# Eight expert units of a top-2 expert layer: wide and small units in turn, or woven chunk by chunk with one load queue each

## The reference

```python
def _moe(h, w_router, w_gate, w_up, w_down):
    logits = (x @ w_router).astype(jnp.float32)
    top_v, top_i = lax.top_k(logits, TOP_K)
    gates = jax.nn.softmax(top_v, axis=-1)
    combine = jnp.sum(jax.nn.one_hot(top_i, N_EXPERTS) * gates[..., None], axis=1)
    for e in range(N_EXPERTS):
        out = out + combine[:, e:e + 1] * _swiglu(x, w_gate[e], w_up[e], w_down[e])
```

## Time and profile before

| | |
|---|---|
| Time, median of 3 runs | 1328.16 us (1327.37 to 1329.48) |
| The profiled execution's own time | 1328.74 us |
| Its span in the trace | 1326.8 us, so 1.94 us lie outside the span |
| Expert layer on PE | from 480.6 us to 1315.6 us |
| PE busy | 1304.6 us (98%) |
| DVE, ACT busy | 795.7 us (60%), 642.6 us (48%) |
| Bytes moved by DMA | 425.50 MB, 321 GB/s over the span |
| Share of the chain that ended last | PE 84%, DVE 9%, ACT 3% |

### The profile page before, as it was taken

One profiled execution on the slowest core, in us unless ns is written; L12 is line 12 of the kernel. 1 busy time (PEld: TensorE's weight loads), 2 busy tenths in 40 slices (PEclk: granted clock), 3 DMA queues, 4 the chain that ended last, 5 costly groups with the idle time before them and its releaser, 6 DMA issues.

```text
span 1326.8 us, 18843 instructions
## 1 busy us (share of the span) xinstructions
PE 1304.6 (98%) x7654; PEld 983.3 (74%) x7654; DVE 795.7 (60%) x957; ACT 642.6 (48%) x672; POOL 4.5 (0%) x12
## 2 busy tenths in 40 slices
PE   9999999999999999999999999999999999999996
PEld 8999999999999977884448885347887345888332
DVE  7564765653888679972129884118885215888122
ACT  6655644352576587761027772017774005776001
POOL 0000000000000000000000000000000000000000
PEclk9999999999999999999999999999999999999998
DMA  7335354463333499999999999999999999999995
GB/s 299 136 128 190 127 191 159 159 220 140 115 143 128 169 377 341 348 376 405 409 411 426 428 427 426 427 399 426 426 427 427 427 405 427 427 427 426 427 426 227
DMA packets 72347, 425.50 MB, mean 321 GB/s; under 512 B 6384, under 2 KB 8432, under 8 KB 27328
## 3 DMA queue, kind: packets, MB, share of 16 engines
q1 hardware_dynamic: 71680, 422.67, 78.7%
q0 software_dynamic: 432, 1.54, 0.3%
q10 hardware_dynamic: 144, 0.02, 0.0%
HBM read 423.16 MB, written 1.05 MB: 320 GB/s over the span
## 4 chain that ended last, share of the span: by engine, by line
PE 84%; DVE 9%; ACT 3%; issue 3%; DMA 1%; SPq 0%; DVEq 0%; ACTq 0%
PE ps L2388 14%; PE ps L2259 7%; PE ps L2260 7%; PE ps L2265 7%; PE ps L2419 7%; PE ps L1720 5%; PE ps L1710 4%; PE ps L1711 4%; PE ps L2284 4%; PE ps L2285 4%; PE ps L2292 4%; PE ps L1758 2%; PE ps L1775 2%; PE ps L1759 2%; DVE wl L1173 1%
## 5 line engine op out<-in xcount | busy, mean ns | idle before, releaser
L1383 DVE TENSOR_TENSOR wl<-raw,wh 128x2048 fp32r<-128x2048 f32 x96 | 218.6, 2289 | 23.9 <-ACT wh L855 23.8
L855 ACT CAST wh<-raw 128x2048 fp32r<-128x2048 f32 x96 | 183.9, 1916 | 66.8 <-PE ps L2260 40.3
L2259 PE MATMUL ps<-wh,gh 128*128 128x512 f32 x448 | 175.3, 391 | 0.7 <-DVE gl L1457 0.7
L2260 PE MATMUL ps<-wh,gl 128*128 128x512 f32 x448 | 174.4, 389 | 0.0
L918 ACT ACTIVATE sil<-ps 64x512 f32<-64x512 f32 x28 | 16.5, 589 | 299.2 <-PE ps L2390 299.2
L2388 PE MATMUL ps<-raw,few 128*64 128x512 f32 x288 | 130.2, 597 | 0.6 <-DMA raw<-in_moe_w_up 0.6
L2390 PE MATMUL ps<-raw,few 128*64 128x512 f32 x288 | 129.5, 597 | 0.0
L2265 PE MATMUL ps<-wl,gh 128*128 128x512 f32 x448 | 119.8, 389 | 0.0
L1596 DVE COPY few_act<-ps 128x256 f32<-128x256 f32 x28 | 11.9, 425 | 177.9 <-PE ps L2402 177.9
L1047 DVE TENSOR_TENSOR wl<-raw,wh 128x4096 fp32r<-128x4096 f32 (+1 forms) x18 | 73.2, 4069 | 61.7 <-ACT wh L614 39.7
L614 ACT CAST wh<-raw 128x4096 fp32r<-128x4096 f32 (+2 forms) x29 | 92.0, 3173 | 34.5 <-PE ps L1711 34.1
(11 more groups left out here) (343 smaller groups left out, 2692.0 us busy)
## 6 DMA issues: line engine op xcount, KB each, us to landing
raw<-in_moe_w_up SPq DMA_DIRECT2D x71, 1024.0 KB, 12.1
raw<-in_moe_w_gate SPq DMA_DIRECT2D x70, 1024.0 KB, 12.1
raw<-in_moe_w_down SPq DMA_DIRECT2D x51, 1024.0 KB, 13.6
unsplit<-in_moe_w_down SPq DMA_DIRECT2D x33, 1024.0 KB, 10.6
unsplit<-in_moe_w_up SPq DMA_DIRECT2D x25, 1024.0 KB, 14.2
unsplit<-in_moe_w_gate SPq DMA_DIRECT2D x22, 1024.0 KB, 17.3
raw_more<-in_moe_w_down SPq DMA_DIRECT2D x15, 1024.0 KB, 11.6
raw<-in_diff_w_qkv SPq DMA_DIRECT2D x8, 1536.0 KB, 6.6
```

The lines of the kernel that those rows point to most:

```text
L855: act.copy(split_piece(wh, p), raw_piece(p, first)).then_inc(wh_ready, 1)
L1383: dve.tensor_tensor(split_piece(wl, p), raw_piece(p, first), raw_f(split_piece(wh, p)), ALU.subtract).then_inc(wl_ready, 1)
L2259: pe.matmul(ps[:, bank, :], gh[:, s], w, start=(k0 + k == 0), stop=False)
L2260: ins = pe.matmul(ps[:, bank, :], gl[:, s], w, start=False, stop=False)
```

## The change

The wide and the small units no longer take turns. They form two streams of 28 chunks each, and one loop of CHUNKS + LAG + 1 = 31 steps runs both: step s takes wide chunk s and small chunk s - 2. Within a step PE goes from one stream to the other: wide gate, small up (first half), small transposes, wide up, small up (second half), half of wide down, wide transposes, half of small down, other half of wide down, other half of small down.

The wide pieces land in six raw slots and SP issues them. The small pieces land in the other five and POOL issues them; the lent places are gone. The first eleven wide pieces still use all eleven slots. The two gathers become one, in four parts of 4 matmuls with 192 moving columns (128 + 64 tokens). The small unit's output is stored as a rounded part above its rest, so that `scatter_few` is one float32r matmul per token tile and half instead of two float32 ones. `sort_experts` moves ahead of the first gathered tokens' low part on DVE. The reserved descriptor space is set to 4096 bytes. The loop that handles more than eight units is kept and does not run here.

Slots and streams:

```diff
-RAW_SLOTS, SPLIT_SLOTS = 11, 3
-LENT = 2 * SPLIT_SLOTS
...
+CHUNKS = WIDE_UNITS * FC
+STREAM = CHUNKS * CPU // FC * 2
+LAG = 2
...
+        wide_ring, few_ring = ROUND[:6], ROUND[6:]
+        held_in = [[("wide", s)] for s in ROUND]
+        for p in range(RAW_SLOTS, STREAM):
+            held_in[wide_ring[(p - RAW_SLOTS) % len(wide_ring)]].append(("wide", p))
+        for p in range(STREAM):
+            held_in[few_ring[p % len(few_ring)]].append(("few", p))
```

The loads, first on SP and then on POOL:

```diff
+            for p in range(STREAM):
...
+                else:
+                    sp.wait_ge(wl_ready, C_MOE + held_in[s][n - 1][1] + 1)
...
+            pool.wait_ge(routed, 1)
+            for p, (kind, i, half) in enumerate(few_pieces):
+                s, n = position["few", p]
+                held, of = held_in[s][n - 1]
+                if held == "wide":
+                    pool.wait_ge(wl_ready, C_MOE + of + 1)
+                else:
+                    pool.wait_ge(few_used, of + 1)
...
+                load_few(before_e if last_of_unit else e, s, kind, i % FC, half)
```

The small unit's output on ACT (DVE subtracts the same way) and the start on DVE:

```diff
+            def few_out(n):
...
+                for h in range(2):
+                    rows_ = slice(h * SMALL, (h + 1) * SMALL)
+                    act.copy(bm["y_few"][rows_, h * BANK:(h + 1) * BANK], ps[rows_, 6, :]).then_inc(few_high, 1)
...
+            sort_experts()
+            gathered_low(1, 0)
+            split(1)
```

On PE:

```diff
+            def gather_part(n, q):
...
+                        ins = pe.matmul(ps[:, 7, k * WITH_FEW:(k + 1) * WITH_FEW], bm["tok"][:, t, (2 * q + k) * P:(2 * q + k + 1) * P],
+                                        bm["pick"][:, t, 0:WITH_FEW], start=(t == 0), stop=(t == QT - 1), skip_group_check=True)
...
+            def scatter_few(n, k, bank=7):
...
+                pe.matmul(ps[:, bank, :], to, bm["y_few"][:, s], start=True, stop=True).then_inc(sc_done, 1)
...
+            for s in range(CHUNKS + LAG + 1):
+                t, n, r = s - LAG, s // FC, s % FC
+                adds = n and s < CHUNKS
+                gathers = r == FC - 1 and n + 1 < WIDE_UNITS
+                if s < CHUNKS:
+                    wide_up(s, "g")
+                if 0 <= t < CHUNKS:
+                    few_up(t, 0)
+                if 1 <= t < CHUNKS:
+                    few_turn(t - 1)
+                if adds and r == 2:
+                    scatter_wide(n - 1, 2)
+                if adds and r == 4:
+                    scatter_few(n - 1, 2)
+                if s < CHUNKS:
+                    wide_up(s, "u")
...
+                if 0 <= t < CHUNKS:
+                    few_up(t, 1)
+                if gathers:
+                    gather_part(n + 1, 0)
+                if 1 <= s <= CHUNKS:
+                    wide_down(s - 1, 0)
+                if s < CHUNKS:
+                    wide_turn(s)
+                if gathers:
+                    gather_part(n + 1, 1)
+                if 1 <= t <= CHUNKS:
+                    few_down(t - 1, 0)
...
+                if 1 <= s <= CHUNKS:
+                    wide_down(s - 1, 1)
+                if gathers:
+                    gather_part(n + 1, 2)
+                if 1 <= t <= CHUNKS:
+                    few_down(t - 1, 1)
...
+            for k in range(2 * QT):
+                scatter_few(FEW - 1, k, 2 + k)
...
-    nc = bacc.Bacc("TRN2", target_bir_lowering=False, num_devices=1)
+    nc = bacc.Bacc("TRN2", target_bir_lowering=False, num_devices=1, dynamic_dma_scratch_size=4096)
```

More of the change, by code:

```diff
@@ L1389, in _ @@
             gap, eg, g1, g2 = one[:, 4], one[:, 5], one[:, 6], one[:, 7]
-            unit_split(0, 0, first=True)
+            split(0)
             dve.wait_ge(route_in, 32)
@@ L1607, in unit_body, with few_out @@
-            def unit_body(u, a, scatter, first=False):
+                    dve.wait_ge(wide_high, 2 * n + h + 1)
+                    dve.tensor_tensor(bm["y_low"][:, s], ps[:, 2 + h, :], raw_f(bm["y_high"][:, s]), ALU.subtract).then_inc(wide_low, 1)
+            def few_out(n):
+                for h in range(2):
+                    s, rows_, other = slice(h * BANK, (h + 1) * BANK), slice(h * SMALL, (h + 1) * SMALL), slice((1 - h) * SMALL, (2 - h) * SMALL)
+                    dve.wait_ge(few_high, 2 * n + h + 1)
+                    dve.tensor_tensor(bm["y_few"][other, s], ps[rows_, 6, :], raw_f(bm["y_few"][rows_, s]), ALU.subtract).then_inc(few_low, 1)
@@ new lines, in wide_turn @@
+            def wide_turn(c):
+                pe.wait_ge(eprod_ready, c + 1)
+                if c:
+                    pe.wait_ge(eal_ready, c)
+                else:
+                    pe.wait_ge(acc_ev, 3)
+                if c >= LAG + 1:
+                    pe.wait_ge(few_act_ready, c - LAG)
+                for k in range(4):
+                    s = slice(k * P, (k + 1) * P)
+                    ins = pe.transpose(ps[:, 4, s], bm["act"][:, s], ident)
+                ins.then_inc(eT_done, 1)
@@ L2244, in unit_body @@
+            for k in range(2 * QT):
+                scatter_few(FEW - 1, k, 2 + k)
+            def unit_body(u, a):
                 gh, gl = bm["gh"], bm["gl"]
@@ L2344, in unit_body @@
                         down(i - 1, (1,))
-                    if first and i == 5:
-                        gather_few(0)
-                        turn_picks(0)
-                    if scatter and i == 3:
+                    if i == 3:
                         pe.wait_ge(pick_ready, u + 1)
@@ L2450, in _ @@
-            for f in range(FEW):
-                unit_body(2 * f, f, False, first=not f)
-                few_body(2 * f + 1, f)
-            for t in range(QT):
-                scatter_few(FEW - 1, t, (SUMS[t], SUMS[2 + t]), 0)
+            pe.nop().then_inc(gathered, 2 * (WIDE_UNITS - 1))
+            pe.nop().then_inc(payT_done, E)
+            pe.nop().then_inc(half_done, E)
             pe.wait_ge(routed, 1)
```

810 lines of the change are left out of this document (466 added, 344 removed).

## The result

The changed kernel takes 1355.67 us (median of 4 runs, 1355.25 to 1355.87), the kernel before 1328.0 us on the same chip: 1.0206 times as long, with a 95% interval of 1.0189 to 1.0224. The forecast was 1336.7 us. The direction was right, the size was not: 27.7 us more instead of 8.5.

The account below looks back on a forecast made before the run. PE was taken to bound the kernel from the end of wide unit 0 on. The terms +21.6, 0, -5.1, -7.9, -1.2, +1.1 and 0 gave +8.5 us on 1328.74, so 1337.2, as median 1336.7 us; range 1322 to 1366.

Parts of the forecast that it names:

- Part 1: PE's extra changes between wide and small matmuls, at 0.21 us into wide and 0.14 back: +21.6 us.
- Rival C: Breaks between wide and small matmuls cost nothing in the weave, so the kernel gets faster: 1315 us, chance 0.12.
- Parts 2 and 4: PE's transposes between matmuls, 1.18 us a chunk before and after: 0; joint gathers at 0.33 us a matmul: 7.9 us saved.
- Part 3: Scatter of small units on PE, 8.8 us before and 3.7 after with float32r matmuls: 5.1 us saved.
- Part 5: PE's waits in wide unit 0, 2.5 us before, half of them taken as saved: 1.2 us less.
- `sort_experts` costs nothing: Moved ahead of the first gathered low part, where DVE idles 3.01 us, it costs nothing; uncovered, 2 us at most.
- Part 6: Between last small matmul and scatter, copies and subtractions take 2.0 us instead of 0.69: +1.1 us.
- Part 7: Loads in the woven units: same bytes, 417 GB/s needed against 427 seen, latency within the allowance: cost 0.
- rival B: POOL's loads bind and PE waits for DMA, slower still: 1350 us, at the far end 1401; chance 0.28.

Follow-up runs that it names:

- b1_scatter: Kernel before with only the new scatter of small units (split output, one float32r matmul a half): 1326.6 us against 1327.4, ratio 0.9991.
- s2_pick_early: Changed kernel with the first pair's picks moved ahead of chunk 1's splits on DVE: 11.0 us less than the changed kernel.
- v1_early_gather: Kernel before with the first small gather behind chunk 1 instead of chunk 5, its picks behind the routing's list: 11.9 us more.
- s1_count_late: Changed kernel with `count_units` behind chunk 0's product on DVE instead of ahead of it: 3.5 us less than the changed kernel.
- v2_routing_early: Kernel before with DVE's sorting, counting and listing placed as in the changed kernel, PE's order kept: costs nothing (0.2 us).
- u1_turn: s3_both with chunk 0's transposes and turned product put behind PE's gate product of chunk 1: 1341.6 us against 1341.8.
- t3_one_queue: s3_both with SyncE issuing the small pieces too, in one order with the wide ones, and GpSimd none: 1342.4 us against 1341.8.
- t2_ups_downs: s3_both with the two halves of each small up product together, and of each small down product too: 1329.0 us, 12.9 less.
- s3_both: Changed kernel with both DVE moves: counting behind chunk 0's product, first pair's picks ahead of chunk 1's splits: 1341.8 us, 13.8 less.
- u2_turn_ups_downs: t2_ups_downs with chunk 0's transposes and turned product put behind PE's gate product of chunk 1: 1329.3 us against 1329.0.

## Why the prediction missed

**Part 1, the breaks** (+21.6): right. The prices were there again (0.34 us for the first wide matmul behind a small one), and taking two round trips away gave back 0.28 and 0.39 us a step, where 0.35 each had been counted. The rule of the Trainium skill, page "TensorEngine Tiling (Array Packing)", section Key Properties, that a change of tiling mode drains the array, stays in agreement with these rows. Rival C (breaks hidden in the weave) is refuted.

**Parts 2 and 4** (0 and -7.9): right in sum. A step with gather takes 24.47 + 9.71 = 34.18 us, a plain one 29.04; a joint gather of 16 matmuls is so 5.1 us, 0.32 each, near the 0.33 taken. The plain step was to be about 28.8; over a whole pair of seven steps only 0.4 us more than forecast are left.

**Part 3** (-5.1): direction right, a little too large; b1_scatter shows 1.2 us a unit where 2.26 - 0.92 = 1.3 were counted.

Together PE's own work grew by 11.8 us instead of 8.6. Some 0.4 us of the difference lie in each woven pair (211.4 against 211), the rest in the first and last steps, where it is not divided.

**Part 5, the waits in wide unit 0** (-1.2): this step failed. Instead of 1.2 us saved, PE waited 8.3 us in its first two steps (3.8 for chunk 0's product, 4.5 for the picks), where all waits of the first wide unit had come to 1.9. The forecast looked at which routing parts DVE still has to do and took their number for their price. It did not ask, for each instruction of PE in the first two steps, when what it waits for is ready. Two things moved. The small gather, in the kernel before behind chunk 5 with its picks long made, came to the end of the second step, ahead of DVE's picks; s2_pick_early gives back 11.0 us by moving the picks alone, and v1_early_gather loses 11.9 us in the kernel before by the early place alone, with a longer wait. And the transposes of chunk 0 lost the gate product that had stood ahead of them, just when the counting was put ahead of the product they need. s1_count_late shows what the counting costs there, 3.5 us. That the lost gate product is the reason stays open: v2_routing_early shows a wait of 1.5 us with that product in place, and u1_turn, which puts it back, saves nothing. "`sort_experts` costs nothing" was right: DVE still had 1.16 us of idle time before the first low part, and v2 moved it for nothing.

**The clock** (no term at all): the second failure. An idle PE cost 8.3 us in two waits, and the lower granted clock behind them 7.0 more. The Trainium skill, page "TensorE: Matmul & The Clock Gate", section Part 1: The HAM clock gate, says that an idle array drops back to half its rate and has to earn the full one again. The trace agrees (0.50 from 520 to 530 us), and a forecast that had found the waits would have had to add it.

**Part 6, the end** (+1.1): near. The wait is 2.1 us as worked out (2.0; against the 0.69 of before that makes 1.3 and not 1.1), the scatter 0.8 shorter; PE also waits 0.5 and 0.3 us for the last down pieces.

**Part 7, the loads** (0): right. In the expert layer there is no wait for DMA before 1332 us, landings are 9 to 13 us, and t3_one_queue shows no price of GpSimd's queue, so rival B is refuted. The Trainium skill, page "DMA: Bandwidth & Descriptors", section Latency and other measured facts, calls engines 7 and 15 usually slower, with GpSimd's descriptors as its guess at the cause; no run here shows a lower rate. t2_ups_downs and b1_scatter saved less than PE's own instructions would give, which fits how near the limit was.

With both moves on DVE the changed kernel takes 1341.8 us, 5.1 above the forecast. That is the forecast's mechanism, with 2 to 4 us of waits and clock left at chunk 0, and the missed work of PE.

## What to carry to other kernels

When an order is rewritten, the steady step is the easy half. Go through the first two or three steps instruction by instruction: what the bounding engine waits for, when that is ready, and which work used to stand ahead of the wait. One gather asked for some 8 us too early cost 12 us, more than half of the 21.6 us counted for 125 extra breaks, because the idle PE paid again in its clock. And before pricing a saving on PE, look how much of it the loads would let through.

## What the hardware showed unexpectedly

- The granted clock fell after short idleness: behind waits of 3.7 to 8.3 us in every profile that had one (the changed kernel, s1_count_late, s2_pick_early, v1_early_gather); behind one of 2.1 us in two profiles out of seven that had one at the start (s3_both, whose stretch 490 to 500 us reads 0.83, and u2_turn_ups_downs), and not in the other five (1.00). Matmuls of no use in the waits kept it at 1.00 and gave back 7.0 us.
- At 1.2 GHz a small gather of 16 matmuls with 64 columns took 7.09 instead of 3.79 us. These matmuls cost nearly as much as those with twice the columns (0.237 and 0.256 us at full clock), and still pay almost double.
- Changes between 128 x 128 float32r and 128 x 64 float32 matmuls cost about a third of a microsecond a round trip, and add up: 0.35 us read in the kernel before, 0.28 and 0.39 us when one was taken out of every step.
- With 178 of 424 MB issued by GpSimd, or all but 1.5 MB by SyncE, the loads reached the same 427 GB/s and the kernels the same time (1341.8 and 1342.4 us).
